# Six gate and up tiles of an FFN taken two at a time, a quarter of the inner dimension by Strassen's scheme

## The reference, cut to what matters

```python
D_MODEL = 2048
SEQ = 256
D_FF = -(-8 * D_MODEL // (3 * 256)) * 256        # 5632
...
x = x + stick_breaking_attention(rms_norm(x, norm_mix), ...)
x = x + swiglu(rms_norm(x, norm_ffn), w_gate, w_up, w_down)
gate = sigmoid(rms_norm(x, ple_norm) @ ple_w_gate)
x = x + gate * (p @ ple_w_proj)
...
def swiglu(h, w_gate, w_up, w_down):
    return (silu(h @ w_gate) * (h @ w_up)) @ w_down
```

## Time and profile before

| | |
|---|---|
| median of 3 runs | 1201.69 us (1201.59 to 1203.84) |
| the profiled execution | 1201.46 us, its span 1199.7 us |
| PE busy | 1194.4 us, 5350 matmuls and transposes |
| DVE busy | 855.3 us |
| ACT busy | 583.4 us |
| read from HBM and written | 232.02 and 7.34 MB, 200 GB/s over the span |

### The profile page before, as it was taken

How to read it: one execution, slowest core, us unless ns; L and a number is a source line. 1 busy time by engine, 2 the same in 40 slices (tenths; PEclk the granted TensorE clock), 3 DMA queues, 4 the chain that set the end, 5 groups by cost and what they waited for, 6 DMA issues and landing times.

```text
span 1199.7 us, 14649 instructions
## 1 busy us (share of the span) xinstructions
PE 1194.4 (100%) x5350; PEld 989.6 (82%) x5350; DVE 855.3 (71%) x1113; ACT 583.4 (49%) x719; POOL 54.5 (5%) x101
## 2 busy tenths in 40 slices
PE   9999999999999999999999999999999999999998
PEld 7878888888888888888888888888888888888887
DVE  5898989899757587686577677667656565656654
ACT  7556475665545644444444444444344444444442
POOL 1302021020000200000000000000000000000000
PEclk9999999999999999999999999999999999999999
DMA  8667576675769766666666676666565656565673
GB/s 281 194 200 210 175 225 194 200 228 177 224 192 284 245 194 183 204 193 187 194 199 186 189 205 194 181 204 196 177 209 180 208 178 208 180 206 176 189 248 108
DMA packets 136298, 240.08 MB, mean 200 GB/s; under 512 B 17026, under 2 KB 24756, under 8 KB 136244
## 3 DMA queue, kind: packets, MB, share of 16 engines
q1 hardware_dynamic: 136212, 239.39, 64.9%
q10 hardware_dynamic: 32, 0.01, 0.0%
HBM read 232.02 MB, written 7.34 MB: 200 GB/s over the span
## 4 chain that ended last, share of the span: by engine, by line
PE 99%; DVE 1%; ACT 0%; issue 0%; DVEq 0%; ACTq 0%
PE acc L1236 94%; PE R L1236 1%; PE Z L1236 1%; PE T L1282 1%; PE acc L1264 1%; DVE w_lo L805 0%; PE T L1302 0%; DVE squares L868 0%; PE acc L1346 0%; PE T L1275 0%; PE Z L1282 0%; PE acc L1418 0%; PE acc L1426 0%; PE Z L1292 0%; PE T L1292 0%; ACT w_hi L542 0%
## 5 line engine op out<-in xcount | busy, mean ns | idle before, releaser
L542 ACT ACTIVATE w_hi<-raw 128x1024 fp32r<-128x1024 f32 x425 | 448.9, 1059 | 534.8 <-PE acc L1236 514.9
L805 DVE TENSOR_TENSOR w_lo<-raw,w_hi 128x1024 fp32r<-128x1024 f32 x425 | 517.1, 1224 | 262.7 <-ACT w_hi L542 260.0
L1236 PE MATMUL acc<-w_hi,xT_hi 128*128 128x512 f32 x1200 | 470.1, 392 | 0.7 <-DVE w_lo L805 0.6
L1236 PE MATMUL acc<-w_hi,xT_lo 128*128 128x512 f32 x1200 | 467.2, 389 | 0.0
L1236 PE MATMUL acc<-w_lo,xT_hi 128*128 128x512 f32 x1200 | 467.0, 389 | 0.0
L1236 PEld LDWEIGHTS acc<-w_hi,xT_hi 128*128 128x128 f32 x1200 | 225.3, 188 | 48.3 <-DVE w_lo L805 2.4
L1236 PEld LDWEIGHTS acc<-w_hi,xT_lo 128*128 128x128 f32 x1200 | 225.2, 188 | 47.6
L1236 PEld LDWEIGHTS acc<-w_lo,xT_hi 128*128 128x128 f32 x1200 | 225.4, 188 | 45.7
L1236 PE MATMUL acc<-w_hi,hT_hi 128*128 128x512 f32 x352 | 136.9, 389 | 0.0
L1236 PE MATMUL acc<-w_lo,hT_hi 128*128 128x512 f32 x352 | 136.9, 389 | 0.0
L1236 PE MATMUL acc<-w_hi,hT_lo 128*128 128x512 f32 x352 | 136.9, 389 | 0.0
(11 more groups left out here) (177 smaller groups left out, 664.3 us busy)
## 6 DMA issues: line engine op xcount, KB each, us to landing
raw<-in_sb_w_in SPq DMA_DIRECT2D x93, 512.0 KB, 4.4
raw<-in_ffn_w_gate SPq DMA_DIRECT2D x88, 512.0 KB, 3.7
raw<-in_ffn_w_up SPq DMA_DIRECT2D x88, 512.0 KB, 3.8
raw<-in_ffn_w_down SPq DMA_DIRECT2D x88, 512.0 KB, 4.1
raw<-in_sb_w_out SPq DMA_DIRECT2D x32, 512.0 KB, 4.7
raw<-in_ple_w_gate SPq DMA_DIRECT2D x32, 512.0 KB, 4.2
w_scratch<-w_blocks SPq DMA_DIRECT2D x16, 192.0 KB, 5.1
w_side<-w_scratch SPq DMA_DIRECT2D x64, 48.0 KB, 2.0
```

What stands on the lines that cost most here:

```text
L542: act.activation(w_parts[0][:, slot(u), 0:n, :], raw[:, slot(u), 0:n, :], ACT.Copy).then_inc(hi_ready, 1)
L805: dve.tensor_tensor(w_parts[1][:, slot(u), 0:n, :], raw[:, slot(u), 0:n, :], w_parts[0][:, slot(u), 0:n, :].bitcast(F32), ALU.subtract).th ...
L1236: last = pe.matmul(acc[pair][tb][:, :], parts[a][:, c, tb * P:(tb + 1) * P], w_parts[w][:, slot(u), i, :], start=(start and i == 0 and n = ...
```

## The change

Tiles 0, 1, 8, 9 and 10 stay as they were. Tiles 2 to 7 are taken as three pairs. A pair has a gate **matrix** and an up matrix of 2048 rows by 1024 columns, and `pair_matrix` runs the six matrices 0 to 5 one after the other, even ones gate, odd ones up. The 16 row blocks are paired as k and k + 8. For two of the eight pairs of row blocks (kind S) the 2 x 2 block product of tokens and weights is computed by Strassen's scheme in Winograd's form with 7 products for 8, for the other six (kind N) by the usual 8. The order is `SNNNSNNN`. An S step has four units, of 6, 6, 6 and 3 matmuls (21), an N step two units of 12 (24). So a matrix has MU = 20 units and 2 x 21 + 6 x 24 = 186 matmuls, where two tiles' gate or up had 16 units and 192.

What it adds and moves:

- **DVE, differences.** Before each S step DVE makes `T13` (one subtraction of 1024 columns) and `T24` (two of 512, the second from the first's result) from the raw weights, in units S_AT-2 and S_AT-1. ACT and DVE split these as they split raw weights.
- **DVE, tokens.** In tile 1 DVE forms the sums and differences of the token blocks (`tokens`, eight operations in units 2 to 9) and splits them with ACT into `tokens_hi` and `tokens_lo`.
- **PSUM.** The products P1 to P8 use all eight banks. After a matrix DVE combines them by eight additions of 512 columns (`combine`): four in units 17 to 19, two in unit 2 and two in unit 3 of the next matrix, behind PE's end of the matrix. ACT copies P1. PE waits on `product_read` before it starts a bank in the next matrix. For an up matrix four multiplications follow in units 4 and 5 of the next, and gate's sigmoid and product (`pair_gate`) lie in units 5 to 16 of the up matrix.
- **Tile 8** starts its gate banks only when both P2 and P4 of matrix 5 have been read.
- **FFN tiles by HBM.** All 11 tiles leave `turn_side`: DVE transposes within blocks (`block_hidden`, two transposes), SP stores 512 KB to HBM (`store_hidden`) and fetches it in four pieces (`fetch_hidden`), ACT and DVE split.
- **Loads.** S steps load whole rows of 1024 columns, two DMAs of 512 KB into slots 0 and 1 of `raw`, once DVE has finished the last unit that used them. N steps use slots 2 and 3 and a new buffer `raw_n`.
- **Loops.** PE's and SP's hardware loop over the tiles is written out.

```diff
+    PAIRS, KH = 3, KD // 2
+    KINDS = "SNNNSNNN"
+    BEFORE_PAIRS, FS = 2, 5
...
-    H_TURN, P_TURN = 0, FN
+    P_TURN = 0
...
+    H_BLOCK, H_STORE, H_FETCH, H_HI, H_LO = 1, 6, 8, 8, 9
+    S_FROM, S_HI, S_LO = 2, 11, 12
+    SIG_AT = 5, 7, 9, 15
...
+            def store_hidden(j):
+
+                sp.wait_ge(h_blocks_ready, TB * (j + 1))
...
+            def fetch_hidden(j):
+
+                sp.wait_ge(h_stored, 16 * (j + 1))
...
+            def load_s(s):
+
+                sp.wait_ge(lo_ready, s_unit(s - 1, 3) + 1 if s > 0 else C2 - 2)
+                for i in range(2):
+                    sp.dma_start(raw[:, i, :, :], pair_columns(s // SM, s % SM + KH * i)).then_inc(s_landed, 16)
...
+            for n in range(NQ):
+                matrix, k = divmod(n, NM)
+                tile = matrix if matrix > 0 else 1
+                s = matrix * SM + k // (NM // SM)
+                if k % (NM // SM) == 0 and s + 1 < SQ:
+                    load_s(s + 1)
+                if n + 2 < NQ:
+                    load_n(n + 2)
+                if matrix % 2 == 0:
+                    if k == 1:
+                        store_hidden(tile)
+                    if k == 2:
+                        fetch_hidden(tile)
+                    if matrix > 0 and k == 3:
+                        store_hidden(tile + 1)
+                    if matrix > 0 and k == 4:
+                        fetch_hidden(tile + 1)
...
-            def hidden(j, u):
-
-                if TURN_AT <= u < TURN_AT + TURN_UNITS:
-                    turn_side(H_TURN + j, u - TURN_AT, TURN_UNITS, 1, C_P1 + j + 1)
-                if u == TURN_LO:
-                    hidden_lo(j)
...
+            def differences(s, part):
+
+                if part == 0:
+                    dve.wait_ge(s_landed, 32 * (s + 1))
+                    dve.tensor_tensor(T13[:, :, :], raw[:, 0:2, 1, :], raw[:, 0, :, :], ALU.subtract).then_inc(differences_ready, 1)
+                else:
+                    dve.wait_ge(differences_ready, 3 * s + 1)
+                    dve.tensor_tensor(T24[:, 0, :], raw[:, 1, 1, :], T13[:, 0, :], ALU.subtract).then_inc(differences_ready, 1)
+                    dve.wait_ge(differences_ready, 3 * s + 2)
+                    dve.tensor_tensor(T24[:, 1, :], raw[:, 1, 0, :], T24[:, 0, :], ALU.subtract).then_inc(differences_ready, 1)
...
+                if v == MU + 2:
+                    dve.wait_ge(unit_used, U0 + MU)
+                    add(part_1 if up else stage[:, 0, :], part_1, P2, product_read[P2])
+                    add(part_b if up else stage[:, 1, :], part_b, P4, product_read[P4])
+                if v == MU + 3:
+                    dve.wait_ge(product_read[P5], 2 * matrix + 2)
+                    add(part_a if up else stage2[:, 0, :], part_a, P3, product_read[P3])
+                    to = junk[:, :] if up else stage2[:, 1, :]
+                    add(to, to, P8, product_read[P8])
...
+                    if matrix % 2 == 0:
+                        tile = matrix if matrix > 0 else 1
+                        if v == 7:
+                            block_hidden(tile)
+                        if v == 14:
+                            hidden_lo(tile)
+                        if matrix > 0 and v == 15:
+                            block_hidden(tile + 1)
...
+                    if j == 1:
+                        if S_FROM <= u < S_FROM + 8:
+                            tokens(u - S_FROM)
+                        if u == S_LO:
+                            tokens_lo()
+                        if u >= CU - 2:
+                            differences(0, u - CU + 2)
+                        if P_FROM <= u < P_FROM + P_STEPS:
+                            turn_p(u - P_FROM)
...
+                    if j == AFTER_PAIRS and k == 0:
+                        for bank in ((P2, P4), (P3, P8))[part]:
+                            pe.wait_ge(product_read[bank], MATRICES)
...
+                for i, factors in enumerate((((P5, s1), (P7, s3)), ((P1, a11), (P2, a12)), ((P6, s2), (P4, a22)), ((P3, s4),))):
+                    U = s_unit(matrix * SM + k, i)
+                    pe.wait_ge(lo_ready, U + 1)
...
-            with nc.Fori(1, FN, engines=[mybir.EngineType.PE], hint_back_edge=True) as j:
+            gate_up(1)
+            pe.wait_ge(tokens_ready, 1)
+            for matrix in range(MATRICES):
```

More of the change, by code:

```diff
@@ new lines, in load_tile, with pair_columns @@
+            def load_tile(j, stores, fetches):
+                for part, w in enumerate((w_gate, w_up)):
+                    for k in range(DU):
+                        u = part * DU + k
+                        load(standard(j)[1] + u, u, D_UNITS[k], w[:, j * NT:(j + 1) * NT])
+                        if u in stores:
+                            store_hidden(stores[u])
+                        if u in fetches:
+                            fetch_hidden(fetches[u])
+            def pair_columns(matrix, c):
+                first = BEFORE_PAIRS + matrix // 2 * 2
+                w = (w_gate, w_up)[matrix % 2]
+                return w[c * P:(c + 1) * P, first * NT:(first + 2) * NT].rearrange("p (a n) -> p a n", n=NT)
@@ L1143, in _ @@
             gate_up(0, first=True)
-            for j in range(1, FN):
+            gate_up(1)
+            for matrix in range(MATRICES):
+                pair_matrix(matrix)
+            for j in range(AFTER_PAIRS, FN):
                 gate_up(j)
@@ new lines, in gate_up, with bank_left @@
+                    products(U0 + u, u, xT, D_UNITS[k], part, k == 0, k == DU - 1, (C_P0, C_P1)[part] + s)
+            def bank_left(matrix, bank):
+                if matrix > 0:
+                    pe.wait_ge(product_read[bank], matrix * (2 if bank == P5 else 1))
+                elif bank in (P2, P4):
+                    pe.wait_ge(acc_free[0][bank == P4], C_P0 + BEFORE_PAIRS)
+                elif bank in (P3, P8):
+                    pe.wait_ge(acc_free[1][bank == P8], C_P1 + BEFORE_PAIRS)
@@ new lines, in eight_products @@
+            def eight_products(matrix, k):
+                for i in range(2):
+                    U = n_unit(matrix * NM + k, i)
+                    c = SM + k + KH * i
+                    pe.wait_ge(lo_ready, U + 1)
+                    for tb, n, bank in ((0, 0, P2), (0, 1, P3), (1, 0, P4), (1, 1, P8)):
+                        first = k == 0 and i == 0 and bank == P8
+                        if first:
+                            bank_left(matrix, bank)
+                        last = three_terms(bank, [a[:, c, tb * P:(tb + 1) * P] for a in xT], U, n, first,
+                                           k == NM - 1 and i == 1)
+                    last.then_inc(unit_used, 1)
@@ L1383, in _ @@
+            gate_up(0, first=True)
+            gate_up(1)
+            pe.wait_ge(tokens_ready, 1)
+            for matrix in range(MATRICES):
+                for k, kind in enumerate(KINDS):
+                    if kind == "S":
+                        seven_products(matrix, KINDS[:k].count("S"))
+                    else:
+                        eight_products(matrix, KINDS[:k].count("N"))
+            for j in range(AFTER_PAIRS, FN):
                 gate_up(j)
```

365 lines of the change are left out of this document (318 added, 47 removed).

## The result

| | before | after |
|---|---|---|
| median of 5 runs | 1202.18 us (1201.59 to 1203.84) | 1195.22 us (1194.80 to 1197.33) |
| ratio | | 0.9946, 95% interval 0.9932 to 0.9959 |
| the profiled execution, its span | 1201.46, 1199.7 us | 1195.22, 1193.3 us |

A forecast was written before the change was run, and what follows sets the result against it. PE, never waiting from 358.52 us on, was taken as the bound. 8.16 - 1.0 - 0.5 - 1.5 - 0.2 = 5.0 us less than 1201.46 gives 1196.5, plus 0.2 for the median: 1196.7 us; range 1194.8 to 1202.5.

The forecast's parts named there:

- 36 matmuls at 0.2267: Six matrices on PE: 1116 matmuls instead of 1152, at 0.2267 us each, take 8.16 us from the path.
- five seams: Between matrices: DVE's additions and lo of unit 4 ready 0.1 to 0.5 us early; 0.2 charged each, 1.0 us.
- entry: Tile 1 into the first S step: late loads hold DVE's differences and lo; 0.5 us, 0 to 2.5.
- exit: Start of tile 8: PE waits until P2 and P4 of matrix 5 are read; 1.5 us, 1.3 to 1.7.
- way through HBM: Matrices 0, 2 and 4: store and fetches take 13.2 us, ACT waits about 1 us; 0.2 us in all.
- turning, loops: PE's and SP's loops written out: nothing to gain; large transposes in place of 16 small ones lighten DVE's load.
- rival of 7 ns a matmul: PE: starting a bank every three matmuls costs what 36 matmuls bring, 7 ns each; result 1201 us; 3%.
- VectorE's intervals: DVE back to back starts operations closer than their durations: 0.60 us for 512 columns, 0.72 if dependent.
- first rival: DVE's bunches aren't covered, each operation taking its duration plus 0.03: costs 8.2 us, 1201.7, or 1199 with half; 20%.
- VectorE as the bound: Matrices: 0.10 us more per DVE operation uses up an even matrix's spare; 0.15 gives 1207.5 us, 0.2 gives 1220; 11%.
- What would show it: Signs in the profile after: 5314 matmuls, 186 in 42.2 us, DVE some 885 us busy, ACT some 608.

The follow-up runs named there:

- eighth product: Changed kernel with P3's three matmuls done twice, so a matrix has 192 matmuls again: 1203.58 us, ratio 1.0013; pair stretch 8.15 us more.
- way through HBM alone: Kernel before with hidden tiles sent through HBM and PE's and SP's loops written out, no block products: 1201.92 us, ratio 1.0005.
- the small transposes: Changed kernel with hidden tiles turned by 16 small VectorE transposes as before, nothing through HBM: 1212.80 us, ratio 1.0094.
- 14.4 us spread: Changed kernel with four more VectorE additions of 512 columns in each matrix, behind lo of units 8, 11, 14 and 17: 1194.86 us, ratio 0.9945.
- 3.6 us at the seams and the exit: Changed kernel with one more VectorE addition of 512 columns behind the four additions at each matrix end: 1198.38 us, ratio 0.9977.
- the run that spent them: Changed kernel with the four HBM fetches done twice for one hidden tile in each of matrices 0, 2 and 4: 1204.41 us, ratio 1.0020.

## Why the prediction was right, step by step

| step | predicted, us | measured, us |
|---|---|---|
| 36 matmuls at 0.2267 | -8.16 | -8.15 (eighth product) |
| five seams | +1.0 (0 to 2.0) | 0.00, margin 0.35 |
| entry | +0.5 (0 to 2.5) | 0.00, 0.39 ahead at unit 20, 1.2 at unit 15 |
| exit | +1.5 (1.3 to 1.7) | +1.67 |
| way through HBM | +0.2 | 0.00, 0.5 to 2.1 ahead, then 1.2 |
| turning, loops | 0 | 0 (way through HBM alone) |
| sum | -5.0 | -6.5 |

The profiled executions differ by 6.24 us, the spans by 6.4; the measured sum is 6.49, and 0.14 of it went to the wait in tile 0. The medians differ by 6.96.

- **The bound.** One price for a matmul was the right reading of the earlier trace rows. It held with eight banks in use, and it also held against the rival of 7 ns a matmul (3%): 1115 intervals average 226.67 ns. The figure of the Trainium skill ("TensorE: Matmul & The Clock Gate"), 215.7 ns, would have given 7.8 us; the eighth product says 8.15.
- **The seam** had the right form and an addend too much. VectorE starts the first addition 0.19 us behind TensorE's next matmul, ready at + 4.41 against + 4.76. The lag was taken as 0.0 to 0.4 behind TensorE's end, and the margin of 0.1 to 0.5 that followed holds the true one of 0.35. The mistake was to charge 0.2 us a seam for a margin that was positive at both ends: a covered step costs nothing, not a mean.
- **VectorE's intervals** decided between the forecast and its first rival (20%). The rival's bunch, 0.72 from start to start, is refuted by the rows of the seam above (0.60). The rule of the Trainium skill ("VectorE: DVE Perf Modes", § The DRAIN you can't avoid), by which the next operation doesn't start until the pipe is empty, doesn't describe these starts: operations that last 0.68 to 0.69 us follow each other after 0.60. What fits is the exception that the same paragraph makes and the prediction left out: "A next op that is not held starts earlier". It gives no figure; here it is 0.08 us.
- **VectorE as the bound** (11%) asked for 0.15 us more per operation, and there are none. Its mechanism is real all the same: the small transposes add more work than that, and there the kernel is 11 us slower than before. Average load and bunch are two limits, as the earlier trace rows were read: 14.4 us spread cost 0.00, 3.6 us at the seams and the exit (3.0 of them at seams) cost 2.35.
- **The entry.** The chain of steps was right to the unit. What was off is the landing time: 5.0 from the earlier trace rows for the second load, where VectorE went on 4.5 us behind its issue (some 0.4 behind that of the first, 454.67). VectorE was ready with unit 15 at 463.35, where 463.7 was forecast, against 464.53 and not 464.7. By the forecast's own times unit 15 was 1 us early and unit 20 only 0.2 (472.0 against 472.2), and it is unit 20 that is tightest in the trace too, by 0.39. The 0.5 was once more a charge on a margin, though here a thin one: by these figures a load that lands 5.0 and not 4.5 us behind its issue would have cost about 0.1 and a little for the stop. The traces of the seven other runs with this entry and the same turning show no stop there either; VectorE waited 2.40 to 2.65 us for the load in all of them.
- **The exit** was sized from two additions, 1.3 to 1.7, and measured 1.59 by the starts. What was missing is 0.09 for matmuls that start further apart behind a stop.
- **The way through HBM.** ACT didn't wait in the pair stretch, where about 1 us was foreseen. The store landed after 5.7 us in the median there, not after the 6.6 of the earlier trace rows.
- **What would show it:** 5314 matmuls, and 42.16 us for 186, were as said; ACT 604.7 for 608. VectorE was busy 870.4, not 885 us: that sum added full durations of 1.22 and 0.69, while the page counts overlapping time once. (The durations alone add up to 29 us more than before, where the forecast's list adds 32.) By matrix, where intervals had been used, 37.65 against 37.6 in the even ones; the odd ones had 33.7 to 36.0 against 35.5.

So the forecast missed by three small charges, 1.7 us on the same side, on steps that its own arithmetic had as covered, less 0.17 at the exit. The 0.2 that it added for the median over the profiled execution wasn't there either. All three margins were then spent in experiments: 0.30 at the seam, 0.39 at the entry, and behind the fetch 0.4 to 2.1 (in the run that spent them), then 1.2.

## What to carry to other kernels

Where the bound engine never waits, price a removed instruction by its start-to-start interval, then write for every other engine a timetable of its bunches against that beat; a step that is ahead by that timetable costs nothing, and one that is late costs its lateness plus 0.1 to 0.2 us. An engine may be 95% busy for free if its work is spread, and cost 0.45 us for a first extra 0.60 us where it is bunched; so move work off the helper engine first, even if that brings nothing by itself. Where a stage ends in an accumulator that must be read, start the next stage in banks that were read long ago: that was worth 1.6 us here for a few lines.
